# Four index-query units of each last layer split into places of their own, and each first index product waiting for the query it reads

## The reference, cut to what matters

```
h = rms_norm(x, norm_g)
proj = einsum('btd,de->bte', h, w_in)
q, k, v, gate_a, u_b, gate_b, q_idx, k_idx, w_idx, merge = split(proj)
q = rope(rms_norm(q, qn_g));  k = rope(rms_norm(k, kn_g))
q_idx = rope(q_idx);          k_idx = rope(k_idx)
s = einsum('bqhd,bkd->bqhk', q_idx, k_idx)
score = einsum('bqhk,bqh->bqk', relu(s), w_idx * idx_scale)   # then masked
_, sel = top_k(score, k_top)          # attention looks at sel alone
attn = softmax(q . k[sel]) . v[sel]
y_a = (attn * silu(gate_a)) @ w_a
y_b = (multiscale_pool(u_b) * silu(gate_b)) @ w_b
x = x + (sigmoid(m_a) * y_a + sigmoid(m_b) * y_b) @ w_out
```

## Time and profile before

| | |
|---|---|
| median of three runs | 1535.16 us (1532.74 to 1535.86) |
| the profiled execution | 1529.96 us, its span 1528.2 us |
| granted clock of TensorE, mean | 0.997 |
| busy: PE, DVE, POOL, ACT | 97%, 61%, 64%, 36% |
| chain that ended last | PE 78%, DVE 13%, POOL 3%, issue 3% |
| layer 0, from K to the first gate unit | about 730 to 804 us |
| layer 1, the same part | about 1131 to 1202 us |

### The profile page before, as it was taken

How to read it: one execution, slowest core, us unless ns; L and a number is a source line. 1 busy time by engine, 2 the same in 40 slices (tenths; PEclk the granted TensorE clock), 3 DMA queues, 4 the chain that set the end, 5 groups by cost and what they waited for, 6 DMA issues and landing times.

```text
span 1528.2 us, 24064 instructions
## 1 busy us (share of the span) xinstructions
PE 1474.9 (97%) x8440; PEld 1193.9 (78%) x8440; DVE 935.7 (61%) x1970; ACT 548.9 (36%) x1253; POOL 974.2 (64%) x1496
## 2 busy tenths in 40 slices
PE   8998998999999999999989999999998999999999
PEld 7776556678777778877989888899996877678777
DVE  7875764676676640037785989644458689774341
ACT  5346664433333310035465343331135523333100
POOL 7533434555665688875886545558889765356795
PEclk9999999999999999999999999999999999999999
DMA  7211000222222332332232211123222221121323
GB/s 260 74 43 42 15 29 28 69 83 96 92 87 95 96 98 95 97 97 74 86 100 82 70 56 60 52 70 119 83 98 84 97 84 56 42 70 56 98 96 110
DMA packets 39694, 123.75 MB, mean 81 GB/s; under 512 B 5680, under 2 KB 8624, under 8 KB 38832
## 3 DMA queue, kind: packets, MB, share of 16 engines
q1 hardware_dynamic: 36912, 114.84, 22.9%
q10 hardware_dynamic: 2688, 7.66, 1.6%
HBM read 118.18 MB, written 4.26 MB: 80 GB/s over the span
## 4 chain that ended last, share of the span: by engine, by line
PE 78%; DVE 13%; POOL 3%; issue 3%; ACT 2%; DMA 1%; SPq 0%; POOLq 0%; DVEq 0%; ACTq 0%
PE ps L844 62%; PE ps L1350 3%; PE ps L863 2%; PE ps L857 2%; DVE score L2570 2%; DVE score L2569 2%; PE ps L968 2%; POOL wlo L708 2%; PE ps L1433 2%; PE ps L1053 2%; POOL whi L704 1%; PE ps L1428 1%; DVE probs L2591 1%; DVE hl L2502 1%; POOL wlo L821 1%
## 5 line engine op out<-in xcount | busy, mean ns | idle before, releaser
L844 PE MATMUL ps<-hh,whi 128*128 128x512 f32 (+1 forms) x1448 | 514.6, 355 | 5.2 <-DVE hl L2358 1.7
L844 PE MATMUL ps<-hl,whi 128*128 128x512 f32 (+1 forms) x1448 | 501.6, 346 | 0.0
L844 PE MATMUL ps<-hh,wlo 128*128 128x512 f32 (+1 forms) x1448 | 500.5, 346 | 0.0
L704 POOL TENSOR_SCALAR whi<-raw 128x256 fp32r<-128x256 f32 x564 | 262.9, 492 | 324.6 <-PE ps L844 321.8
L708 POOL TENSOR_TENSOR wlo<-raw,whi 128x256 fp32r<-128x256 f32 x564 | 440.2, 811 | 11.8
L844 PEld LDWEIGHTS ps<-hh,whi 128*128 128x128 f32 x1448 | 272.6, 188 | 65.5 <-issue 18.0
L844 PEld LDWEIGHTS ps<-hh,wlo 128*128 128x128 f32 x1448 | 272.8, 188 | 34.9
L844 PEld LDWEIGHTS ps<-hl,whi 128*128 128x128 f32 x1448 | 272.7, 188 | 31.8 <-issue 1.0
L801 POOL TENSOR_TENSOR wlo<-raw,whi 128x256 fp32r<-128x256 f32 x160 | 134.8, 873 | 92.7 <-ACT whi L1737 92.7
L844 PE MATMUL ps<-plain_high,whi 128*128 128x264 f32 (+2 forms) x232 | 74.0, 319 | 6.6 <-POOL wlo L708 6.3
L844 PE MATMUL ps<-plain_high,wlo 128*128 128x264 f32 (+2 forms) x232 | 72.0, 311 | 0.0
(11 more groups left out here) (383 smaller groups left out, 2702.9 us busy)
## 6 DMA issues: line engine op xcount, KB each, us to landing
raw<-in_w SPq DMA_DIRECT2D x196, 512.0 KB, 3.5
kept<-x ACTq DMA_DIRECT2D x2, 1056.0 KB, 6.0
x<-kept ACTq DMA_DIRECT2D x2, 1056.0 KB, 7.1
raw<-in_w SPq DMA_DIRECT2D x16, 128.0 KB, 2.7
out<-x SPq DMA_DIRECT2D x8, 256.0 KB, 4.5
raw<-in_w SPq DMA_DIRECT2D x6, 256.0 KB, 3.2
raw<-in_w SPq DMA_DIRECT2D x4, 384.0 KB, 3.2
x<-in_x SPq DMA_DIRECT2D x2, 512.0 KB, 8.0
```

The lines of the kernel that those rows point to most:

```text
L704: ins = pool.tensor_scalar(whi[s][:, c:c + PIECE], raw[s][:, c:c + PIECE], 1.0, 0.0, ALU.mult, ALU.add)
L844: mm = pe.matmul(out, lhs, rhs, start=start and n == 0, stop=stop and n == 2)
```

## The change

The list of units with places of their own now holds all four index-query units of each layer. c = 0 keeps its place; c = 1 goes to `bl`, c = 2 to `bh`, c = 3 to `al`. POOL splits all four with `split_extra`, with no wait for a use, and only in layer 0 with one wait, for the last chunk of x of the block before, ahead of c = 2. The units c = 4 and c = 5 go to `whi` and `wlo` and wait for the use of K and V, which had these places last. From c = 6 on nothing is changed. PE reads the parts from the new places, and ahead of each index pair it waits for the one query that the pair reads.

```
--- before.py
+++ after.py
@@ -271,12 +271,16 @@
 
         MLP_EXTRA = U_GU + 2
         PLE_EXTRA = [U_PLE + PLE_C + m for m in range(4)]
-        QUERY_EXTRA = [U_LAYER + l * L_UNITS + 2 for l in range(LAYERS)]
+        QUERY_EXTRA = [U_LAYER + l * L_UNITS + 2 + c for l in range(LAYERS) for c in range(4)]
 
         def extra_part(n, low, k, count=1):
 
             if n in QUERY_EXTRA:
-                return (query_low if low else query_high)[:].rearrange("p k m -> p (k m)")[:, k * P:(k + count) * P]
+                c = QUERY_EXTRA.index(n) % 4
+                if c == 0:
+                    return (query_low if low else query_high)[:].rearrange("p k m -> p (k m)")[:, k * P:(k + count) * P]
+                first = DC * P * low + k * P
+                return (bl, bh, al)[c - 1][:].rearrange("p c t -> p (c t)")[:, first:first + count * P]
             if n in PLE_EXTRA:
                 m = PLE_EXTRA.index(n)
                 c, low = ((16, 18)[low], True) if m == 3 else (8 + 2 * m + 2 * low, low)
@@ -822,14 +826,21 @@
                                              ple_part(u - PLE_C, False, c).bitcast(F32), ALU.subtract)
                 ins.then_inc(ty.sem("unit_split"), 1)
             elsewhere += DC
-            for l, n in enumerate(QUERY_EXTRA):
+            for l, n in enumerate(QUERY_EXTRA[0::4]):
                 for s in range(2):
                     split(n // 2 - 1, s, False)
                 if l:
                     pool.wait_ge(*at("gated_a", (l - 1, plans[l - 1]["slots"] - 1)))
                 split_extra(n)
-                split(n // 2, 1, False)
-                with pool.Fori(n // 2 + 1, (n + L_UNITS) // 2 - 1) as i:
+                split_extra(n + 1)
+                if l == 0:
+                    pool.wait_ge(*at("x_new", ("ple", DC - 1)))
+                split_extra(n + 2)
+                split_extra(n + 3)
+                for s in range(2):
+
+                    split(n // 2 + 2, s, False, unit_ready(n - 2 + s))
+                with pool.Fori(n // 2 + 3, (n + L_UNITS) // 2 - 1) as i:
                     for s in range(2):
                         split(i, s, False)
 
@@ -1272,8 +1283,8 @@
                         pe.wait_ge(*free)
                     for tok, (lo, n) in enumerate(cols2(l)):
                         for k in range(DC):
-                            if c == 0:
-                                mm = unit_extra(QUERY_EXTRA[l], out[:, tok, 0:n], k, plain_high[:, k, lo:lo + n],
+                            if c < 4:
+                                mm = unit_extra(QUERY_EXTRA[4 * l + c], out[:, tok, 0:n], k, plain_high[:, k, lo:lo + n],
                                                 plain_low[:, k, lo:lo + n])
                                 continue
                             mm = three(out[:, tok, 0:n], high[:, k], low[:, k], plain_high[:, k, lo:lo + n],
@@ -1373,8 +1384,8 @@
                     if c == 4:
 
                         pe.wait_ge(*at("v_out", l))
-                        pe.wait_ge(*at("q_ready", (l, 3)))
                     if c >= 4:
+                        pe.wait_ge(*at("q_ready", (l, c - 4)))
                         index(*plan["early"][c - 4][1])
                 g_free = [None, None]
```

## The result

The changed kernel is faster. Its four executions took 1520.91 to 1526.70 us, median 1524.62, against 1534.66 for the kernel before (its three runs and one more). The ratio is 0.9927, 95% interval 0.9907 to 0.9947. That is 11.2 us less (8.1 to 14.3), where 7.8 were forecast. The medians themselves lie 10.0 us apart; without the profiled execution and the extra run of before they are 1523.92 and 1535.16 us, whose ratio is 0.9927. With so few executions one more or less on each side moves the result by 1 us.

A forecast was written before the change was run, and what follows sets the result against it. PE's own work fills three quarters of the span; the savable time was six waits for POOL and DVE, about 9 us. Layer 0's 4.2 plus layer 1's 3.7 gave 7.9 us off the median: 1527.4 us, range 1523.5 to 1532.0.

The forecast's parts named there:

- The six waits: PE's waits for POOL and DVE between c = 2 and c = 5 in layers 0 and 1, about 9 us.
- Layer 0: Start of layer 0: c = 5 starts 4.3 us earlier; 0.1 us taken off at c = 7, giving 4.2 us.
- Layer 1: Start of layer 1: c = 5 starts 4.9 us earlier; after later POOL waits, 3.7 us remain.
- the term for c = 3: Layer 1: PE waits for ACT's copies of c = 1, ending at 1164.02, so c = 3 starts at 1164.1.
- second rival: Key chain slips: POOL's work costs DVE its full 3.1 us, delaying c = 3; total gain 3.1 us, 1532.1; chance 0.13.
- The reading of the full block: POOL 23.25 and DVE 23.79 busy of 24 us read as mutual slowing in direction, not a full block.
- the give-back at c = 6 and c = 7: Layer 1: PE waits for POOL's splits again, 0.7 us at c = 6 and 0.5 us at c = 7.
- The two edits are worth something only together: Earlier splits alone: index pair still stands until about 780, gain nearly nil; both edits together 4.3 us in layer 0.
- POOL as the bound: Rival: every split from 742.26 on takes 7.9 us, PE goes at POOL's pace, 4.0 us slower, 1539.2; chance 0.04.
- The gain of layer 1: Rival: later DVE selection steps bind in layer 1, only layer 0's 4.2 us stay, 1531.0; chance 0.10.
- The clock's case: Rival: shorter waits at the layers' starts also remove a clock fall worth 3.0 us, 10.9 in all, 1524.3; chance 0.10.
- from the sum to the median: Whole kernel: 7.9 us taken off the runs' median, small DVE slowing rounded in, 1527.4 us; range 1523.5 to 1532.0.

The follow-up runs named there:

- ACT's new order: Changed kernel, with ACT taking the product of c = 1 out of PSUM before making the first high part of h; ratio 0.9940, measured again 0.9938.
- after_third: The changed kernel with no edit, measured again in 12 executions on the same chip as the re-measured ACT order; ratio 0.9951, 1521.20 to 1534.71 us.
- filled waits: Kernel before, with PE multiplying into a bank nobody reads during its six waits; ratio 1.0006, mean clock 0.9951.
- the waits alone: Kernel before with its two places kept, each index pair waiting only for the one query it reads; ratio 0.9992.
- places alone: Changed kernel with its four places, but the first index pair waiting for the fourth query as before; ratio 0.9995.
- three places: Changed kernel without the place in al, c = 3 and c = 4 split into the common places; ratio 0.9989.

## Why the prediction was right, and where it was not

**What bounds, and the mechanism: right.** The six waits are gone, POOL was done with c = 3 at 759.2 (forecast near 757, and all marks of layer 0 lie 2.4 us later in this execution), and it waits for PE ahead of c = 6. The index pair came 31.79 us behind the first product of c = 0; the forecast was 31.6 (776.2 less 744.57).

**Layer 0: 4.2 us forecast, 4.19 measured.** Two small errors met in it: c = 3 came 0.3 us later than forecast (19.92 us behind c = 0, not 19.6), and the units behind it took a little less.

**Layer 1: 3.7 forecast, 4.23 measured, by two errors against each other.** The first is the term for c = 3: it came 0.8 us later than forecast (19.93 us behind c = 0, not 19.2). The second rival was at work there in small. DVE's first rows of the key in layer 1, and POOL's low part of c = 3 and high part of c = 4 beside them:

```profile
1152.79 3.45 DVE L2537 RECIPROCAL score<-score 128x528 f32<-128x528 f32 x1
1156.28 1.30 DVE L2540 TENSOR_TENSOR kT<-probs,score 64x528 f32<-64x528 f32 x1
1157.59 0.81 DVE L2542 TENSOR_TENSOR kiT<-probs,keep 64x528 f32<-64x528 f32 x1
1158.41 0.81 DVE L2540 TENSOR_TENSOR kT<-probs,score 64x528 f32<-64x528 f32 x1
1159.23 0.81 DVE L2542 TENSOR_TENSOR kiT<-probs,keep 64x528 f32<-64x528 f32 x1
...
1154.20 2.82 POOL L726 TENSOR_TENSOR al<-raw,al 128x256 fp32r<-128x256 f32 x4
1156.97 3.33 POOL L708 TENSOR_SCALAR whi<-raw 128x256 fp32r<-128x256 f32 x4
```

The row that took 0.70 us takes 1.30 beside the end of POOL's split of c = 3. The next took 0.81 instead of 0.70, and the pair of operations behind the four 1.96 instead of 1.61. ACT's swapped copies of c = 1 ended 19.78 us behind c = 0 instead of 19.09, and PE waited 1.03 us for them. The full 3.1 us of that rival never came: the moved splits lay beside the reciprocal, and there neither engine slowed the other (a split took 4.4 us beside it and 4.4 with DVE idle; the reciprocal took 3.45 us, and one of the kernel before, with POOL mostly idle, 3.44).

**The reading of the full block: wrong.** The prediction took "POOL was busy 23.25 and DVE 23.79 of the same 24 us" as a sign against a full block. But a row's time may hold what its engine stood for behind the other, so two engines that both show as busy can be taking turns, and the rows above look like that. The DVE row of 1156.28 ends at 1157.58, 0.56 us behind the end of POOL's last tensor_tensor at 1157.02. From there on DVE's rows start every 0.82 us, and POOL's four tensor_scalar operations take 0.83 us each. Alone they took 0.38 us each, and a DVE row 0.70. The Trainium skill (page "SBUF — State Buffer", section "SBUF: two separate sides") has the block last for one instruction at a time, and only against DVE operations with two SBUF inputs or in a two-port mode. The trace agrees with that, so far as equal pace shows it; no run here tests it by itself. The step from this rule to "paid by one of the two engines whole" did not follow, since the moved splits lay mostly beside the reciprocal, which has one input.

The second error is the give-back at c = 6 and c = 7, which I priced at 1.2 us. It did not happen, since the split of c = 6 took 7.06 us (1176.31 to 1183.37) and not 7.9. PE came to c = 6 at 1183.43. It needed no wait by 0.06 us, so this was close; in the version with ACT's new order, where PE comes earlier, the wait of 0.4 us is there.

**The halves: right in the result.** "The two edits are worth something only together" holds: 0.9995, 0.9992, and 0.9927 to 0.9951 together. The reason I gave for the first half, DVE's query at the old time, was not the one: DVE came 1.6 us earlier in layer 0, and in the profile the clock took that.

**The rivals.** POOL as the bound did not come: the mean of the five splits was 6.1 us, below 7.75. The gain of layer 1 arrived: the span of `after_third` is 8.5 us shorter. The clock's case, 1524.3, was near the first measurement, but the runs do not bear it out: filling the same waits brought at most about 2 us, falls in the kernel before moved the marks by 0.2 us at most, and the later ratios are 0.9943 and 0.9951.

**The number.** The sum itself was 0.5 us too small: its term for what c = 6 and c = 7 give back in layer 1 was 1.2 us and measured nothing, and the late c = 3 took most of that back. The step that failed is the last: from the sum to the median, and its range. I took the scatter of the kernel as 3 us from three runs of before, and let the range end at the clock's case. In truth single executions of one kernel differ by 7.6 us, and by 13.2 in the 23 of before that were measured beside the filled waits (1528.88 to 1542.09), and the mean clock goes along: those of the changed kernel at 0.997 and above took 1520.91 to 1523.92 us, its slowest, 1534.71, was among those of lower clock. The medians of the three series of the changed kernel, of 4, 6 and 12 executions, differ by 2.4 us themselves (1524.62 to 1527.03). Their ratios give 11.2, 8.7 and 7.5 us less than before (0.9927, 0.9943, 0.9951), the differences of the medians 10.0, 6.4 and 7.7. The sum of 7.9 lies among them, as does the 8.4 that the marks show, and all three intervals hold 8.4. So the 2.8 us by which the first ratio goes beyond 8.4 were luck of a few executions, as far as the runs tell. A low end for a change worth 8 us should have reached 2 us further down.

**What stays open.** Why the clock falls behind one wait in one execution and not in the next was not tried. A fall at about 1250 to 1265 us is in two of the three profiles of the changed kernel and in none of the three of the kernel before, but also in those of the waits alone and the waits filled; whether the change has a part in it is not shown. Whether the moved waits of places alone and of three places would cost less with PE kept busy was not tried either.

## What to carry to other kernels

Where one engine prepares operands for another at changing speed, look for the time at which it stands idle just before it becomes too slow. More places let it work then, and the gain is the whole train of waits, but only if the next waits in line are made as narrow as the data they guard. Take the other's waits away all at once or not at all: one wait of 2 to 3 us cost as much here as three that add up to 4.

When the clock moves single executions by more than the change is worth, compare distances between two marks of the program in one profile with the same distance in the other. In the changed kernel they repeated to 0.05 us and before to 0.2, where the whole time went up and down by 7. Then see in a pair of profiles with the same falls of the clock whether the gain reaches the end.

## What the runs showed of the hardware that was not expected

The granted clock fell to 0.50 behind waits of PE of 1.8 and 2.0 us in some executions and not in others (ahead of c = 4: two profiles of the kernel before of three). It fell behind the waits of 2.4 and 3.0 us of places alone and behind the 2.2 us of three places, and not behind the 1.8 us there. A fall costs about 1.6 us where PE has work that others wait for, and nearly nothing where PE would have waited anyway. So a higher mean clock need not mean a time shorter by as much: with its waits filled the kernel before had the higher clock (0.9951 against 0.9940), for which the fit above would give 1.1 us, and its mean span was 0.4 us shorter, which is within the noise.

POOL's split and DVE's operations with two inputs made each other longer, 7.9 us against 4.4 for a split and up to 1.30 against 0.70 for a DVE row. They went at one pace, a DVE row every 0.82 us beside POOL operations of 0.83, and both engines then show as busy all the time. By contrast, a reciprocal of 3.45 us beside a split slowed neither.
